# Turning nine of the compression's twelve tiles between the sample tile's products

## What is computed

```python
def compress(raw, pe, w1, w2):
    B, S = raw.shape[:2]
    n = S // CMP_BLOCK                                   # blocks of 32 rows
    x = raw.reshape(B, n, CMP_BLOCK, 2, N_KV, HEAD_DIM) + jnp.transpose(pe, (1, 0, 2))[:, :, None, :]
    x = jnp.transpose(x, (0, 1, 3, 4, 2, 5)).reshape(B, n, 2, N_KV, CMP_BLOCK * HEAD_DIM)
    hdn = jax.nn.gelu(jnp.einsum('bnsgf,sfh->bnsgh', x, w1))
    return jnp.einsum('bnsgh,shd->bnsgd', hdn, w2)
```

## Time and profile before

| what | us |
|---|---|
| median of 3 runs | 1307.87 (1305.82 to 1318.08) |
| the profiled execution | 1307.76 |
| its span, as the profiler sees it | 1305.9 |
| outside that span | 1.86 |

### The profile page before, as it was taken

The page is one execution under the profiler, slowest core; times in us unless marked ns, Lnnn a source line. Parts: engine busy times, 40 slices in busy tenths (PEclk is TensorE's granted clock), DMA queues, the critical chain, the costliest instruction groups (busy, mean ns, idle before and its releaser), DMA issues. The chain is left out here.

```text
span 1305.9 us, 21830 instructions
## 1 busy us (share of the span) xinstructions
PE 1177.4 (90%) x8090; PEld 888.1 (68%) x8091; DVE 721.3 (55%) x1430; ACT 545.9 (42%) x949; POOL 127.0 (10%) x184
## 2 busy tenths in 40 slices
PE   4899999999879999999989982899999999999844
PEld 2467766666766677777757862677888887888721
DVE  0212222222447576777767767887665588585247
ACT  0110110100246677666543224665464467464135
POOL 0101021000010000000000001021010012010051
PEclk8799999999888999999999995899999999999967
DMA  9934454220228830000043326999667789793578
GB/s 360 319 134 155 154 214 78 45 77 14 77 90 302 228 80 2 2 2 2 2 138 123 140 100 239 359 384 380 250 226 279 257 301 384 257 360 144 233 280 154
DMA packets 91125, 239.06 MB, mean 183 GB/s; under 512 B 7770, under 2 KB 15709, under 8 KB 90887
## 3 DMA queue, kind: packets, MB, share of 16 engines
q1 hardware_dynamic: 76821, 192.10, 43.1%
q0 software_dynamic: 9296, 31.06, 7.6%
q10 hardware_dynamic: 4930, 14.85, 2.9%
HBM read 199.94 MB, written 44.33 MB: 187 GB/s over the span
## 5 line engine op out<-in xcount | busy, mean ns | idle before, releaser
L2376 PE MATMUL psum<-w_hi,x_parts 128*128 128x512 f32 x736 | 240.0, 398 | 6.9 <-DVE x_parts L2500 6.0
L2493 DVE TENSOR_TENSOR w_lo<-raw,w_hi 128x2048 fp32r<-128x2048 f32 x95 | 213.3, 2287 | 52.0 <-ACT w_hi L2435 51.5
L2435 ACT CAST w_hi<-raw 128x2048 fp32r<-128x2048 f32 x90 | 167.6, 1914 | 59.1 <-DVE work L2511 50.0
L633 PE MATMUL psum<-low,top 128*128 128x512 f32 (+5 forms) x640 | 189.1, 467 | 1.7 <-ACT top L764 1.7
L2376 PEld LDWEIGHTS psum<-w_hi,x_parts 128*128 128x128 f32 x736 | 139.7, 190 | 38.3 <-issue 9.2
L633 PEld LDWEIGHTS psum<-low,top 128*128 128x128 f32 (+1 forms) x640 | 105.4, 182 | 69.6 <-issue 60.1
L2376 PE MATMUL psum<-w_lo,x_parts 128*128 128x512 f32 x368 | 144.5, 393 | 0.0
L2376 PE MATMUL psum<-w_hi,a_parts 128*128 x368 | 120.6, 399 | 5.2 <-DVE a_parts L2506 5.1
L1581 DVE CUSTOM_DVE_ANT_0 low<-psum,high 128x512 f32<-128x512 f32 (+5 forms) x172 | 92.2, 579 | 37.8 <-PE psum L1271 24.8
L1467 ACT ACTIVATE low<-low,high 128x640 f32<-128x640 f32 (+9 forms) x140 | 98.9, 710 | 10.2 <-DVE high L1581 10.0
L1301 PE MATMUL psum<-keep,low 128*128 128x128 f32 (+1 forms) x556 | 93.2, 287 | 10.8 <-ACT high L1528 6.3
(11 more groups left out here) (367 smaller groups left out, 1451.8 us busy)
## 6 DMA issues: line engine op xcount, KB each, us to landing
raw<-in_moe_w_gate SPq DMA_DIRECT2D x16, 2048.0 KB, 11.4
raw<-in_moe_w_up SPq DMA_DIRECT2D x16, 2048.0 KB
raw<-in_moe_w_down SPq DMA_DIRECT2D x16, 2048.0 KB
high<-in_w_mod SPq DMA_DIRECT2D x11, 2048.0 KB, 12.9
y_d<-work ACTq DMA_DIRECT2D x24, 512.0 KB, 6.9
high<-in_x_prompt SPq DMA_DIRECT2D x16, 512.0 KB, 3.7
y_d<-high SPq DMA_DIRECT2D x1, 8192.0 KB
low<-in_w_in SPq DMA_DIRECT2D x3, 2048.0 KB, 16.8
```

Source lines behind the costliest of these rows:

```text
L633: mm = pe.matmul(c.bank(2 + n % 2)[lo:lo + T, 0:wide], hT[i % 2][:, k, 0:T], c.w_in[:, k, at:at + wide], start=(k == 0), stop=(k == KT - 1))
L2376: mm = pe.matmul(out, left[l][:, k * P:(k + 1) * P], w[:, bass.ds(at - o + k * step, 512)], start=n == 0, stop=n == len(steps) - 1)
L2435: act.copy(c.w_hi[:, at:at + PART // 2], c.raw[:, o:o + PART // 2]).then_inc(hi_done[p], 1)
L2493: dve.tensor_tensor(low, c.raw[:, o:o + PART // 2], c.w_hi[:, at:at + PART // 2].bitcast(F32), ALU.subtract).then_inc(c.lo_done[p], 1)
```

## The change

Three functions take the place of the loops: `copy_pairs` (ACT), `turn_pairs` (PE) and `add_places` (DVE) do what was said above for one tile n. They are called for n = 0 to 8 (`EARLY_TILES` = 9) among the steps of the sample tile, on all three engines, and for n = 9 to 11 where all twelve were. The added rows go to columns 0 to 767 of `w_in` (chunks 0 and 1, which the sample tile has then read), in four parts of 192 columns, so the addition is four instructions of 128 x 128 elements for a tile, not two of 128 x 256. w1 goes to columns 1280 to 1791 (chunk 2's) in four DMAs of 512 KB, which ACT issues behind the square root of the sample tile, without the wait for the last queries. The prompt rows are read back to `page_nat[0..3]`, each as soon as the copy of that tile is done. `peT`, `hid` and w2 move to memory of the modulation vectors, and ACT waits (`mods_out`) before its first copy.

```diff
@@ block_projection, sync: the read back of the prompt rows
-            sp.wait_ge(q_done, NT)
             for n in range(4):
+                sp.wait_ge(c.paired, n + 1)
                 for s in range(2):
                     sp.wait_ge(kv_out[s], kv_dmas[2 * n + s])
...
-                sp.dma_start(c.cmp_rows[n].rearrange("p q a d -> p (q a d)"), src).then_inc(c.cmp_rows_in[n], 16)
+                sp.dma_start(c.page_nat[n].rearrange("p q a d -> p (q a d)"), src).then_inc(c.cmp_rows_in[n], 16)
@@ tensor
+                if i == smp:
+                    turn_pairs(c, pe, 0)
+                    turn_pairs(c, pe, 1)
                 if i >= 1:
                     pool_window(last)
                 chunk(i, 2)
+                if i == smp:
+                    turn_pairs(c, pe, 2)
+                    turn_pairs(c, pe, 3)
                 if i >= 1:
                     pool_mix(last)
...
                 chunk(i, 3)
+                if i == smp:
+                    turn_pairs(c, pe, 4)
...
             queries(smp, (0,))
+            turn_pairs(c, pe, 5)
             keys(smp)
             queries(smp, (1,))
+            turn_pairs(c, pe, 6)
             pool_window(smp)
             queries(smp, (2,))
+            turn_pairs(c, pe, 7)
             pool_mix(smp)
             queries(smp, (3,))
+            turn_pairs(c, pe, 8)
             gating(smp)
@@ scalar
+                if i == smp:
+                    act.wait_ge(c.mods_out, 64 * 4)
+                    copy_pairs(c, act, 0)
+                    copy_pairs(c, act, 1)
                 act.wait_ge(z_ready, 4 * i + 1)
...
+                if i == smp:
+                    copy_pairs(c, act, 2)
+                    copy_pairs(c, act, 3)
                 act.wait_ge(z_ready, 4 * i + 3)
...
+                    copy_pairs(c, act, 4)
                     act.wait_ge(z_ready, 4 * i + 4)
...
                 act.wait_ge(st_ready, i + 1)
                 act.activation(rstd[0:T, :], mv[0:T, 1:2], ACT.Sqrt).then_inc(sqrt_done, 1)
-            act.wait_ge(q_done, NT)
             act.dma_start(c.cmp_w2, t["cmp_w2"][0].rearrange("s h d -> h s d")).then_inc(c.cw_in, 16)
-            act.dma_start(c.cmp_w1, t["cmp_w1"][0].rearrange("s (c p) h -> p s c h", p=P)).then_inc(c.cw_in, 16)
-            act.wait_ge(c.mods_out, 64 * 4)
+            for part in range(4):
+                src = t["cmp_w1"][0, part // 2].rearrange("(c p) h -> p c h", p=P)[:, 8 * (part % 2):8 * (part % 2) + 8, :]
+                act.dma_start(c.w_in[:, :, KV0 + P * part:KV0 + P * (part + 1)], src).then_inc(c.cw_in, 16)
+            for n in range(5, EARLY_TILES):
+                copy_pairs(c, act, n)
             compression_scalar(c, act)
@@ vector: behind the copy of the sample tile's v columns: add_places 0, 1; behind the pooled
@@ product of tile 7: 2, 3; behind its gating: 4; behind the norm of the sample tile's v: 5;
@@ behind the sample tile's keys: 6; behind its pooled sums: 7; behind its pooled product: 8
+def add_places(c, dve, n):
+    dve.wait_ge(c.nt_ps, n + 1)
+    if n == 0:
+        dve.tensor_copy(c.peT, c.bank(4)[:, 0:32].rearrange("p (s c) -> p s c", s=2)).then_inc(c.pe_ev, 1)
+        dve.wait_ge(c.pe_ev, 1)
+    at = 8 * CMP_TILES[n]
+    for part in range(4):
+        s, half = part // 2, part % 2
+        a = dve.tensor_tensor(
+            both_rows(c, part).rearrange("p c (g n) -> p c g n", g=2)[:, :, :, at:at + 8],
+            c.bank(n % 2)[:, 2 * s * P:(2 * s + 2) * P].rearrange("p (g n c) -> p c g n", g=2, c=CB // 2)[:, 8 * half:8 * half + 8],
+            c.peT[:, s, 8 * half:8 * half + 8].unsqueeze(2).unsqueeze(3).to_broadcast([P, 8, 2, 8]), ALU.add)
+    a.then_inc(c.nt_ev, 1)
@@ compression_tensor
-    for n in range(len(CMP_TILES)):
+    for n in range(EARLY_TILES, len(CMP_TILES)):
+        turn_pairs(c, pe, n)
     pe.wait_ge(c.nt_ev, len(CMP_TILES))
-    pe.wait_ge(c.cw_in, 32)
+    pe.wait_ge(c.cw_in, 80)
```

More of the change, by code:

```diff
@@ L276, in setup @@
     c.pe_n, c.pe_in = c.misc[:, 144:272], early_sem("pe_in")
[L277 to L280, removed]
+    c.cmp_w2 = view(ZR_ + 3248, 2, HD)
     c.cw_in = early_sem("cw_in")
@@ L890, in _ @@
                                     c.bank(7, 256).rearrange("p (b t) -> p b t", b=2)[:, :, 0:T]).then_inc(kT_evac, 1)
+                    if i == NT:
+                        add_places(c, dve, 6)
                 if i < NT:
@@ L898, in _ @@
                         dve.tensor_copy(zuv[i % 2][0:Ti, 1, P:], c.bank(3)[NS:P, 0:P]).then_inc(z_dve, 1)
+                        add_places(c, dve, 0)
+                        add_places(c, dve, 1)
                 if i >= 1:
@@ L904, in _ @@
                         .then_inc(pd_evac, 1)
+                    if i == NT:
+                        add_places(c, dve, 7)
                     dve.wait_ge(po_ready, i)
@@ L913, in _ @@
                         mod_vector(c, dve, i + 1)
+                    if i == smp:
+                        add_places(c, dve, 2)
+                        add_places(c, dve, 3)
+                    if i == NT:
+                        add_places(c, dve, 8)
                     bias = c.sgu_b if last < smp else c.sgu_bS
@@ L921, in _ @@
                     dve.tensor_tensor(c.sgo[0:T, :], c.sgo[0:T, :], zuv[last % 2][0:T, 0, :], ALU.mult).then_inc(sgo_ready, 1)
+                    if i == smp:
+                        add_places(c, dve, 4)
                     dve.wait_ge(so_ready, i)
@@ L939, in _ @@
                     dve.tensor_tensor(vn, vn, c.lnv_b[0:Ti, :], ALU.add).then_inc(vn_ready, 1)
+                    if i == smp:
+                        add_places(c, dve, 5)
                 if i < smp:
@@ L949 @@
 CMP_TILES = tuple(range(4, 4 + NB)) + tuple(range(4))
+EARLY_TILES = 9
 def compression_places(c):
-    c.xcT = c.view(W_, 2, CB // 2, 2 * NBLK)
-    o = W_ + 2 * (CB // 2) * 2 * NBLK + 2 * (CB // 2) * P + 4 * 512 + 2 * P
     c.pairs = [c.view(ZR_ + 1792 + 512 * s, 4, 2, HD) for s in range(2)]
-    c.peT = c.view(o, 2, CB // 2)
-    c.hid = c.view(o + 32, 2, 2, NBLK)
-    assert o + 32 + 4 * NBLK <= MIX_
+    c.peT = c.view(ZR_ + 2816, 2, CB // 2)
+    c.hid = c.view(ZR_ + 2848, 2, 2, NBLK)
     c.kcS = c.view(C2_, NBLK)
@@ L966, in compression_places, with both_rows @@
     c.gate_done = c.sem("gate_done")
-def compression_tensor(c, pe):
-    pe.wait_ge(c.pe_in, 16)
-    pe.transpose(c.bank(4)[:, 0:32], c.pe_n[0:32, :], c.ident[0:32, 0:32]).then_inc(c.pe_ps, 1)
-    for n in range(len(CMP_TILES)):
[L974 to L980, removed]
+def both_rows(c, part):
+    return c.w_in[:, :, 2 * NBLK * part:2 * NBLK * (part + 1)]
@@ new lines, in turn_pairs, with copy_pairs @@
+def turn_pairs(c, pe, n):
+    if n == 0:
+        pe.wait_ge(c.pe_in, 16)
+        pe.transpose(c.bank(4)[:, 0:32], c.pe_n[0:32, :], c.ident[0:32, 0:32]).then_inc(c.pe_ps, 1)
+    pe.wait_ge(c.paired, n + 1)
+    if n >= 2:
+        pe.wait_ge(c.nt_ev, n - 1)
+    for sg in range(4):
+        mm = pe.transpose(c.bank(n % 2)[:, sg * P:(sg + 1) * P],
+                          c.pairs[n % 2][:, sg, :, :].rearrange("p q d -> p (q d)"), c.ident)
+    mm.then_inc(c.nt_ps, 1)
+def copy_pairs(c, act, n):
+    tile = CMP_TILES[n]
+    if tile < 4:
+        act.wait_ge(c.cmp_rows_in[tile], 16)
+    else:
+        act.wait_ge(c.page_nat_in[tile - 4], 16 * NPAGE)
+    if n >= 2:
+        act.wait_ge(c.nt_ps, n - 1)
+    act.copy(c.pairs[n % 2], c.page_nat[tile % 4 if tile < 4 else tile - 4].rearrange("p q a d -> p a q d")).then_inc(c.paired, 1)
@@ L981, in compression_tensor @@
+def compression_tensor(c, pe):
+    for n in range(EARLY_TILES, len(CMP_TILES)):
+        turn_pairs(c, pe, n)
     pe.wait_ge(c.nt_ev, len(CMP_TILES))
-    pe.wait_ge(c.cw_in, 32)
+    pe.wait_ge(c.cw_in, 80)
     for s in range(2):
         for k in range(CB // 2):
-            mm = pe.matmul(c.bank(2 + s)[:, 0:2 * NBLK], c.cmp_w1[:, s, k, :], c.xcT[:, s, k, :],
+            part = 2 * s + k // 8
+            w1 = c.w_in[:, k % 8, KV0 + P * part:KV0 + P * (part + 1)]
+            mm = pe.matmul(c.bank(2 + s)[:, 0:2 * NBLK], w1, both_rows(c, part)[:, k % 8, :],
@@ L986, in compression_tensor @@
                            start=(k == 0), stop=(k == CB // 2 - 1))
         mm.then_inc(c.hid_ps, 1)
-    pe.wait_ge(c.pe_ev, 1)
     pe.wait_ge(c.hid_ev, 1)
@@ L1026, in compression_vector @@
     dve.memset(c.vc2, 0.0).then_inc(c.zeroed, 1)
[L1027 to L1037, removed]
+    for n in range(EARLY_TILES, len(CMP_TILES)):
+        add_places(c, dve, n)
     dve.wait_ge(c.kc_ps, 1)
```

## The result

The changed kernel takes 1.0057 times the time of the kernel before (95% interval 1.0031 to 1.0083): medians of 1318.2 us (8 runs, 1311.76 to 1320.33) and 1312.2 us (8 runs, 1305.82 to 1318.08). The ratio is that of the fast runs: without the slowest run of the kernel before, the median of its other seven is 1310.8 us. A later measurement gave 1.004 (1.0011 to 1.007). So it is slower, by 0.4 to 0.6% in the two measurements, 5 to 7.5 us. The runs of either kernel lie over more than 8 us.

What follows compares the result with a forecast made beforehand. PE was taken as the bound, busy for 90% of the span, except in some 13 us three engines share badly. Later products, +3.6, and clock, +2.5, gave +6.1 on 1307.8: 1313.9, stated as 1314 us, range 1304 to 1321.

Steps and rivals of the forecast that it cites:

- Five turns ahead of the queries: On PE, turns n = 0 to 4 ahead of the sample tile's first queries cost 2.75 us, entries included.
- Turn 5 waits for ACT: PE stands still 8.3 us behind queries 0, until ACT's copy 5, queued behind five DMA issues, ends at 352.7 us.
- From turn 5 to the end of gating_out: On PE in the sample tile: 8.2 us at full clock, plus four turns 2.4 and addition 8 1.0, makes 11.6.
- Three turns left: Turns 9 to 11 and their additions: products wait for additions, not w1's load, and start at 368.9 against 365.32, +3.6 us.
- The clock: PE at low clock when turn 5 starts, slowing the first 5 to 6 us: +2.5 us, bounds 0 and 7.
- the low clock stays: Rival: PE stays at half clock through the turns and half of the products, +14.5, 1322 us; chance 0.10.
- Issues are short: Rival: ACT's queue takes all five weight issues without blocking, turn 5 at 349.3, total 1309.9 us; chance 0.25.
- Faster: Rival: copy 5 nearly in time without low clock, 1304.9 us, or attention's half clock ends 10 us earlier; chance 0.12.
- The signs: Right: PE gap 7 to 9 us, third and fourth w1 issues 2 to 4 each, additions 0.28, products at about 371.
- one sign of being wrong: A change behind the barrier, or in the clock of the attention's first 20 us, larger than the one ahead of the products.

Runs made afterwards that it cites:

- the run with copies 5 and 6 first: The change with copies 5 and 6 on ACT ahead of the five weight issues; stretch 55.10 us, ratio 1.0020 to the kernel before.
- The run with two queues: The change with two quarters of w1 issued by ACT and two by SP; stretch 55.72 us, ratio 1.0022 to the kernel before.
- the gap filled: The change with 54 spare transposes on PE ahead of turn 5; stretch 57.54 us, ratio 1.0037 to the kernel before.

## Why the prediction was right

The forecast was +6.1 us (1314, range 1304 to 1321 on a base of 1307.8); measured were +5.1 in the profile's stretch (+9 between the first profile of before and the second of the change) and +5 to +7.5 in time, 1318.2 us. Of the base only the median moved with more runs, from 1307.9 to 1312.2.

- *Five turns ahead of the queries, 2.75 with entries.* The first quarter of the queries ended 19.96 us into the stretch, before 17.15: +2.81. Additions of 128 x 128 took 0.21 each in a row (eight in 1.68) against the 0.25 taken.
- *Turn 5 waits for ACT.* Right in place and cause, and shown by the run with copies 5 and 6 first. The square root came 3.4 us later, as said. The size was too large: five issues took 5.1 us and not 6.5, and the gap was 6.57 and not 8.3. The term at fault is the blocking of the third and fourth issue, taken at 2.6 and 2.1, measured at 1.86 and 1.55. The run with two queues shows that it is blocking. But it does not last until the first and the second quarter have landed, as I took it: ACT was free 1.7 and 1.8 us ahead of that. What frees it is not shown, and three quarters took between 4.20 and 5.54 us with the same list of ACT.
- *From turn 5 to the end of gating_out.* 12.4 us (346.32 to 358.71), forecast 11.6 and part of the clock. With the gap filled it is 10.4 (346.36 to 356.80), so 1.95 of it is the clock, and the 11.6 was 1.2 too long. Most of that is addition 8 in front of the last gating, taken at 1.0: the wait ahead of gating_out went only from 0.96 to 1.15.
- *Three turns left.* 4.5 from there to the products, forecast 0.7 + 3.8. That the load of w1 is off the path and the additions end last was right.
- *The clock, +2.5 ahead of the products.* That held, by an estimate from two rows: the 1.95 above, and 0.4 in the last three turns (3.76 us from turn 9 to the products, 3.33 where the clock was full). What the sum lacks is another 2.33 in the products. I had priced that as part of the rival "the low clock stays" (0.10). In this profile it is a second fall, behind the small waits around the last three turns, and it came in the run without the gap as well.
- *Luck.* The sum has the products 46.7 us into the stretch; they started at 43.43. So it was 3.3 us too long ahead of them, half of it the gap, and 2.33 too short in them. The two errors nearly cancel.
- *Rivals.* "Issues are short" falls with the 4.64. "Faster" needed five issues for nothing. What turns the sign in the stretch is the order on ACT together with a busy PE, not cheaper issues. "The low clock stays" came in part in the second profile of the change: half clock for some 17 us, and again from the last turns into the products, which makes +9.2 in the stretch against its +14.5.
- *The signs.* The gap's releaser, DVE ahead of the products and the half clock behind the gap came as said. The gap (6.57, 6.38) missed its 7 to 9, the third and fourth quarter (1.86, 1.55) their 2 to 4, the additions (0.21) their 0.28. Counted from the sample tile, the products started some 3 us ahead of the 371, and at it in the second profile. And one sign of being wrong came: the time behind the barrier changed by 5.0 us, more than the 2.8 ahead of the products. It tells nothing, since the kernel before moved by 14.8 there between its own two profiles; one profile of each kernel could not have carried that test.

The Trainium skill (DMA: Bandwidth & Descriptors, Issuing engines are not separate DMA queues) says that starting a DMA is usually short beside the transfer. Here two quarters agree (about 0.6 us each, landing after 4.8 and 5.9), the third and fourth (1.86 and 1.55, landing after 7.3 and 6.9) do so less.

## What to carry to other kernels

Before work is moved between the steps of a busy engine, follow the helper that feeds it through everything queued ahead on its own engine, transfer issues too: one DMA cut into four cost its issuer five times as much here (4.64 against 0.87). Put what another engine waits for ahead of the issues. And where PE must wait for some us, count the clock behind the wait as part of its price; here the early turns with the right order on ACT brought at most 1 us in the stretch, and spare work in the waits behind them another 3.7.

## What was not expected of the hardware

- The granted clock fell behind several waits of 0.6 to 1.2 us each as well as behind one long one: 0.50 at 362 to 364, where PE had been busy for 0.87, 1.37 and 1.02 of 2 us.
- With nearly the same gap, 6.57 and 6.38 us, the half clock lasted about 7 us in one profile and some 17 in the other. Of these 4.6 and 12.6 lie behind the gap, where PE was busy throughout in both.
- A small transfer of 8 KB behind two of 512 KB on one queue took 1.63 us to issue, against 0.3.
- The third and fourth of four transfers on one queue held their issuer, but let it go 1.7 and 1.8 us before the first and second had landed.
